# Two of four pairs of memory values made during the norms between layers, and the SSD gate unit moved between the two output halves

## What is computed

```python
for layer in range(DEPTH):
    kind, idx = layer % N_MIXERS, layer // N_MIXERS
    g = P['norm_g'][layer]
    h = rms_norm(x, g[0])
    ...
    x = x + rms_norm(y, g[1])
    h = rms_norm(x, g[2])
    y = memory_cross_attn(h, mem_k[layer], mem_v[layer], P['x_w_q'][layer], P['x_w_o'][layer])
    x = x + rms_norm(y, g[3])

def memory_kv(mem, g, w_k, w_v):
    m = rms_norm(mem, g)
    shp = mem.shape[:2] + (X_HEADS, X_HEAD_DIM)
    return (m @ w_k).reshape(shp), (m @ w_v).reshape(shp)
```

## Time and profile before

| | |
|---|---|
| median of 3 runs | 2404.57 us (2403.11 to 2412.82) |
| the profiled execution, its own time | 2406.28 us |
| its span in the profile | 2404.5 us |
| mean granted TensorE clock | 0.905 of full speed |
| PE, POOL, DVE, ACT busy | 92%, 52%, 53%, 41% of the span |
| DMA | 321.35 MB, 134 GB/s over the span |

### The profile page before, as it was taken

The page is one execution under the profiler, slowest core; times in us unless marked ns, Lnnn a source line. Parts: engine busy times, 40 slices in busy tenths (PEclk is TensorE's granted clock), DMA queues, the critical chain, the costliest instruction groups (busy, mean ns, idle before and its releaser), DMA issues.

```text
span 2404.5 us, 37822 instructions
## 1 busy us (share of the span) xinstructions
PE 2215.2 (92%) x14852; PEld 2014.2 (84%) x14852; DVE 1270.4 (53%) x2173; ACT 980.6 (41%) x1585; POOL 1245.1 (52%) x1565
## 2 busy tenths in 40 slices
PE   6899999789999999899799999999899889989997
PEld 5888997688899997797698889888799679889976
DVE  5798334246666675434245555555233428983342
ACT  3677433423344432333433223332143347774422
POOL 4798881343344452471363334444377039988812
PEclk8999999988899997799898888888799999999998
DMA  3444576143334323376223332333366524435760
GB/s 112 148 123 132 177 242 204 48 118 99 92 113 124 110 92 109 125 245 203 79 88 108 108 107 86 97 98 100 122 205 230 179 76 139 134 118 176 250 202 26
DMA packets 329760, 321.35 MB, mean 134 GB/s; under 512 B 21512, under 2 KB 311216, under 8 KB 329584
## 3 DMA queue, kind: packets, MB, share of 16 engines
q1 hardware_dynamic: 328720, 318.60, 41.7%
q10 hardware_dynamic: 864, 0.34, 0.1%
HBM read 289.27 MB, written 29.61 MB: 133 GB/s over the span
## 4 chain that ended last, share of the span: by engine, by line
PE 65%; DVE 18%; ACT 5%; DMA 5%; issue 3%; POOL 1%; SPq 1%; ACTq 0%; DVEq 0%
PE ps L677 10%; PE ps L678 9%; PE ps L682 9%; PE ps L1208 4%; PE ps L687 3%; PE ps L667 3%; PE ps L668 3%; PE ps L669 3%; PE ps L1084 2%; DVE work L2071 2%; PE ps L1253 2%; PE ps L945 2%; PE ps L954 2%; DVE work L1921 2%; POOL wl L1403 1%
## 5 line engine op out<-in xcount | busy, mean ns | idle before, releaser
L1403 POOL TENSOR_TENSOR wl<-raw,wh 128x256 fp32r<-128x256 f32 x1536 | 1240.6, 843 | 1124.2 <-ACT wh L1426 1123.0
L677 PE MATMUL ps<-Hh,wh 128*128 128x320 f32 (+1 forms) x1536 | 488.0, 334 | 57.5 <-DVE Hl L1967 26.1
L1426 ACT ACTIVATE wh<-raw 128x1024 fp32r<-128x1024 f32 (+1 forms) x400 | 399.7, 1020 | 331.1 <-DMA raw<-hg_w_in 85.1
L678 PE MATMUL ps<-Hl,wh 128*128 128x320 f32 (+1 forms) x1536 | 473.1, 324 | 0.0
L677 PEld LDWEIGHTS ps<-Hh,wh 128*128 128x128 f32 x1536 | 315.4, 205 | 82.0 <-issue 47.9
L678 PEld LDWEIGHTS ps<-Hl,wh 128*128 128x128 f32 x1536 | 317.3, 207 | 1.3
L1921 DVE TENSOR_SCALAR work<-ps 128x512 f32<-128x512 f32 (+9 forms) x248 | 116.1, 486 | 272.2 <-PE ps L1100 56.1
L682 PE MATMUL ps<-Hh,wl 128*128 128x320 f32 (+1 forms) x1536 | 254.7, 309 | 2.8 <-POOL wl L1403 2.8
L682 PEld LDWEIGHTS ps<-Hh,wl 128*128 128x128 f32 x1536 | 233.5, 193 | 4.1 <-POOL wl L1403 4.1
L667 PE MATMUL ps<-Oh,wh 128*128 128x320 f32 x512 | 168.9, 330 | 9.1 <-POOL wl L1403 5.0
L668 PE MATMUL ps<-Ol,wh 128*128 128x320 f32 x512 | 164.8, 322 | 0.0
(11 more groups left out here) (406 smaller groups left out, 4112.4 us busy)
## 6 DMA issues: line engine op xcount, KB each, us to landing
raw<-rg_w_in SPq DMA_DIRECT2D x128, 256.0 KB, 3.7
raw<-hg_w_in SPq DMA_DIRECT2D x128, 256.0 KB, 5.0
raw<-ssd_w_in SPq DMA_DIRECT2D x96, 256.0 KB, 3.8
work<-cache_mem_k SPq DMA_DIRECT2D x40, 512.0 KB, 6.5
raw<-rg_w_out SPq DMA_DIRECT2D x64, 256.0 KB, 3.6
raw<-x_w_k SPq DMA_DIRECT2D x64, 256.0 KB, 3.6
raw<-x_w_v SPq DMA_DIRECT2D x64, 256.0 KB, 5.5
raw<-x_w_q SPq DMA_DIRECT2D x64, 256.0 KB, 3.6
```

Of the source, the lines that this page charges most:

```text
L677: pe.matmul(ps[:, bank, 0:n], high(half, k), mh[:, k, 0:n], start=(k == 0), stop=False)
L678: pe.matmul(ps[:, bank, 0:n], high(half, k), ml[:, k, 0:n], start=False, stop=False)
L1403: ins = pool.tensor_tensor(out, src, wh[:, n % HALVES, r:r + 2].bitcast(F32), ALU.subtract)
L1426: act.activation(wh[:, n % HALVES, 0:rows], raw[:, slot, 0:rows, half * P:(half + 1) * P], ACT.Copy).then_inc(hi_ready, 1)
```

## The change

Layers 1 to 3 get the first two of their four value pairs (`AHEAD = 2`) at the end of the layer before:

- **Units.** Each attention but the last is followed by 4 units (`NEXT_AT`), the two pairs of the next layer; attentions of layers 1 to 3 have 28 of their own. The places move by 4.
- **The early memory norm.** After the attention's last cache block is used, DVE scales the memory rows by the next layer's gains and makes `Hl`; ACT makes `Hh` inside its loop over the output units. The full memory norm stays where it was.
- **The pairs.** PE runs pair 0 (bank 4) behind the sums of the first norm, then four sums of the second, the first half of pair 1 (bank 5), four sums, the second half. ACT copies each to `at_ahead` and the next `high` waits until both are used.
- **DRAM.** SP stores the two pairs to `mv` during the next mixer (`store_ahead`) and loads them back into `at_v` in the next attention. Before it no value weights are put for heads 0 and 1.
- **Attention of layers 1 to 3.** Pairs 2 and 3 alone; the sums of the query norm stand behind pair 2.
- **SSD.** PE: `outputs(j, 0)` ahead of `take_z(i, 1)`. DVE: fading and `outputs(j, 0)` ahead of the gate.
- Waits that keep the shared places apart (`at_ahead_read`, `at_ahead_out`, `at_ahead_back`). Norms are numbered by functions in place of `3 * L + ...`; this alone changes nothing.

The core of the diff:

```diff
+MIX_UNITS = 8 * GROUPS
+MIX_AT = [0, 100, 196, 308]
+OUT_AT = 260
+ATT_AT = [64, 164, 276, 372]
+AHEAD = 2
+QUERY_AT = [80, 176, 288, 384]
+NEXT_AT = [96, 192, 304, 400]
...
+def values_of(L):
+    return range(AHEAD if L else 0, XH)
...
         @block.sync
...
+            def store_ahead(L):
+                sp.wait_ge(*past("at_ahead_read", AHEAD * L))
+                sp.dma_start(RES["mv"][L, 0, :, 0:AHEAD, :].rearrange("(a p) h d -> p a (h d)", p=P), at_ahead).then_inc(S("at_ahead_out"), 16)
...
                 for n in range(EARLY):
                     cache(n)
+                if layer:
+                    sp.wait_ge(*past("at_ahead_out", 16 * layer))
+                    sp.dma_start(at_v[:, :, 0:256 * AHEAD], RES["mv"][layer, 0, :, 0:AHEAD, :].rearrange("(a p) h d -> p a (h d)", p=P)).then_inc(S("at_ahead_back"), 16)
                 for h in range(XH):
-                    put(cols_of(A["x_w_v"][layer], h * 256))
+                    if h in values_of(layer):
+                        put(cols_of(A["x_w_v"][layer], h * 256))
                     sp.wait_ge(*past("at_k_ready", layer * XH + h + 1))
                     sp.dma_start(RES["mk"][layer, 0, :, h, :].rearrange("(a p) d -> p a d", p=P), at_k[:, h % 2]).then_inc(S(f"at_k_out{h % 2}"), 16)
...
+                if layer < DEPTH - 1:
+                    for h in range(AHEAD):
+                        put(cols_of(A["x_w_v"][layer + 1], h * 256))
...
         @block.tensor
...
+                    if j >= 0:
+                        outputs(j, 0)
                     if projects:
                         take_z(i, 1)
                     if j >= 0:
-                        outputs(j, 0)
                         outputs(j, 1)
...
-                for p in range(XH):
-                    values(p)
-                    if p == 0:
+                for p in values_of(L):
+                    pe.wait_ge(*past("at_kvt_ready", KD * L + p + 5))
+                    values(p, p)
+                    if p == values_of(L)[0]:
                         turn_memory(3)
                         sum_squares(3 + 4 * L, 7)
...
                 if L < DEPTH - 1:
-                    sum_squares(5 + 4 * L, 7)
+                    pe.wait_ge(*past("h_ready", KD * (ahead_norm(L + 1) + 1)))
+                    values(0, 4)
+                    for k in range(4):
+                        sum_square(5 + 4 * L, 7, k)
+                    values(1, 5, (0,))
+                    for k in range(4, KD):
+                        sum_square(5 + 4 * L, 7, k)
+                    values(1, 5, (1,))
...
         @block.scalar
...
+                q0 = QUERY_AT[L]
                 ahead(a0 + KD + 2)
                 root(3 + 4 * L, 7)
                 ahead(a0 + KD + 4)
-                high(3 * L + 2)
-                ahead(a0 + KD + 6)
-                ahead(a0 + KD + 8)
+                high(query_norm(L), out=Oh)
+                ahead(q0 - 2)
+                ahead(q0)
...
                 for t in range(KD):
-                    upto(a0 + 24 + t + 2)
-                    act.wait_ge(used, a0 + 24 + t + 1)
+                    upto(q0 + KD + t + 2)
+                    if L < DEPTH - 1:
+                        high_part(ahead_norm(L + 1), t, memh, Hh, NMEM)
+                    act.wait_ge(used, q0 + KD + t + 1)
...
                 root(4 + 4 * L, 6)
                 if L < DEPTH - 1:
+                    def take_ahead(p):
+                        act.wait_ge(used, NEXT_AT[L] + 2 * p + 2)
+                        act.activation(at_ahead[:, :, 256 * p:256 * p + 256], ps[:, 4 + p, :].rearrange("p (a d) -> p a d", a=2), ACT.Copy).then_inc(S("at_ahead_read"), 1)
                     x_squares(2 * L + 1)
+                    take_ahead(0)
+                    ahead(NEXT_AT[L] + 2)
                     root(5 + 4 * L, 7)
-                    high(3 * L + 3)
+                    high(mixer_norm(L + 1), free=NEXT_AT[L] + 4)
+                    take_ahead(1)
+                    ahead(NEXT_AT[L] + 4)
...
         @block.vector
...
                     pack(i)
-                    gate(i)
                     if j >= 0:
                         fade(j)
                         outputs(j, 0)
+                    gate(i)
+                    if j >= 0:
                         outputs(j, 1)
...
+                if L < DEPTH - 1:
+                    wait("at_kb_used", 32 * L + 32)
+                    memory_norm(L + 1, ahead_norm(L + 1), memh)
                 residual(4 + 4 * L, gain(L, 3))
```

More of the change, by code:

```diff
@@ L50, with ahead_norm, mixer_norm, memory_norm_of @@
 EXP_SET = "natural_log_exp_and_others"
[L53 to L56, removed]
+MIX_UNITS = 8 * GROUPS
[5 more added lines that the diff above has]
+NEXT_AT = [96, 192, 304, 400]
+def ahead_norm(L):
+    return 4 * L - 1
+def mixer_norm(L):
+    return 4 * L
+def memory_norm_of(L):
+    return 4 * L + 1
+def query_norm(L):
+    return 4 * L + 2
+def values_of(L):
+    return range(AHEAD if L else 0, XH)
+def values_count(L, p):
+    return L * (XH - AHEAD) + p + 1 if L else p + 1
 N_UNITS = 400
@@ L423, in rg @@
                 u(1)
-                sp.wait_ge(*past("h_ready", KD * (1 if l == 0 else 10)))
+                sp.wait_ge(*past("h_ready", KD * (mixer_norm(3 * l) + 1)))
+                if l:
+                    store_ahead(3)
                 if l == 0:
@@ L746, in take_ri @@
                     pe.wait_ge(*past("rg_u_ready", g0 + i + 1))
+                    if l and i == 0:
+                        pe.wait_ge(*past("at_ahead_read", 3 * AHEAD))
                     if g0 + i:
@@ L771, in take_out @@
                     done(mm)
-                fresh.append(KD * (0 if l == 0 else 9))
+                fresh.append(KD * mixer_norm(3 * l))
                 take_u(0)
@@ L1197, in memory, with values @@
                     project(n % 4, n % 2, n=NMEM)
-                def values(p):
-                    halves(2)
-                    pe.wait_ge(*past("at_kvt_ready", KD * L + p + 5))
+                def values(p, bank, parts=(0, 1)):
+                    if 0 in parts:
+                        halves(2)
                     both, rest_of = pair(), pair_low()
-                    for a in range(2):
+                    for a in parts:
                         at = slice(a * P, (a + 1) * P)
@@ L1456, in root, with high_part, high @@
                 act.activation(rs[:, 0:width], rs[:, 0:width], ACT.Exp, scale=-0.5).then_inc(S("rs_ready"), 1)
-            def high(n, free=None):
+            def high_part(n, k, src, out, width=NT):
+                act.wait_ge(*past("h_full", KD * n + k + 1))
+                act.activation(out[:, k, 0:width], src[:, k, 0:width], ACT.Copy).then_inc(S("h_high"), 1)
+            def high(n, src=Y, out=Hh, width=NT, free=None):
                 if free is not None:
@@ L1463, in high @@
                 for k in range(KD):
-                    act.wait_ge(*past("h_full", KD * n + k + 1))
-                    w = NMEM if n % 3 == 1 else NT
-                    src = (memh if n != 4 else memh_ssd) if n % 3 == 1 else Y
-                    out = Oh if n % 3 == 2 else Hh
-                    act.activation(out[:, k, 0:w], src[:, k, 0:w], ACT.Copy).then_inc(S("h_high"), 1)
+                    high_part(n, k, src, out, width)
             for name, how, tile, r0 in rows:
@@ L1716, in ssd @@
                 ahead(u + 4)
-                high(4, u)
+                high(memory_norm_of(1), memh_ssd, Hh, NMEM, u)
                 squares_of(7)
@@ L1948, in log1p, with normal @@
                 sync()
-            def normal(n, root, src, g, dst=None, width=NT):
-                dst = Y if dst is None else dst
+            def normal(n, root, src, g, dst=Y, width=NT, h=Hh, l=Hl):
                 for k in range(KD):
@@ L2117, in o_low @@
                     wait("rg_o_high", g0 + i + 1)
+                    if l and i == 0:
+                        wait("at_ahead_out", 48)
                     tt(Ol16[:, 2 * i:2 * i + 2, :], rg_o, Oh16[:, 2 * i:2 * i + 2, :].bitcast(F32), SUB).then_inc(S("rg_o_ready"), 1)
-                wait("h_ready", KD * (1 if l == 0 else 10))
+                wait("h_ready", KD * (mixer_norm(3 * l) + 1))
                 for b in range(2):
@@ L2358, in hg @@
                 r16 = restart[:, SEQ:SEQ + 16]
-                wait("h_ready", 7 * KD)
+                wait("h_ready", KD * (mixer_norm(2) + 1))
                 did(dve.memset(hg_A[:, :, 0:1], 0.0))
@@ L2407, in finish @@
                     sync()
+                    if i == 0:
+                        wait("at_ahead_out", 32)
                     did(copy(Oh16[:, 2 * i:2 * i + 2, :], hg_o))
```

80 lines of the change are left out of this document (48 added, 32 removed).

## The result

The changed kernel took **2446.08 us** (median of 4, 2439.66 to 2448.25), the kernel before 2407.78 beside it (4 runs). The ratio is **1.0147**, 95% interval 1.0115 to 1.0179: 38.3 us slower by the medians. The forecast was 2424, 16 to 19 slower; the range ended at 2443, three short of the median. The profiled execution took 2439.66 (span 2437.9), the fastest of the four; the profiled one of before had 2404.5, so 33.4 between the traces.

The account below looks back on a forecast made before the run. PE, busy 92% of the span, bounds the kernel, so time goes where it lacks work or runs at the lower clock. 25 - 1.5 + 14 - 18 = +19.5 gives 2425.8 profiled, 2424 median; range 2392 to 2443.

Parts of the forecast that it names:

- place 2: Attention of layers 1 to 3: a longer chain of weight puts, landings and key copies delays the query units, +14 us.
- Place 1: Norms after layers 0, 1, 2: two pairs moved in start each mixer 8.3 us later, three times, +25 us.
- Normalising takes 4.8: Query norm in layer 2's attention: the step between the root and the first `Ol`, taken as 4.8 us.
- The upper bound of this place, 24: Attention of layers 1 to 3: range 0 to +24 us, by weight landings of 3.7 to 7 us each.
- The wait of 5.1: Norms after layers 0, 1, 2: PE stands 5.1 us in pair 1 until its second unit is split.
- The bound of 9.0: Norms after layers 0, 1, 2: upper bound of each mixer's delay, 9.0 us, with the half pair at half rate.
- Place 3, SSD: SSD groups: reordering shortens PE's stretches at 1.2 GHz, saving 18 us, bounds 0 to -34.
- 3 + 3 + 2 + 4 x 2.7: SSD: savings in us over the seven groups that project and have a group behind them, put at -18.
- the fall behind the small instructions: SSD: clock fall after the 5.8 us stretch of small instructions ahead of the gate unit, charged 1 us.
- The rival in which the chip gives only half of it: SSD: clock falls ahead of the gate unit in every group, SSD gives -9, total +28.5, 2433 us; chance 0.2.
- HGRN: -1.5 forecast: HGRN's first group: four units split at mixer start, not three, so the 1.8 us wait for POOL mostly goes, -1.5.
- The early pairs pay: Attention of layers 1 to 3: value weights arrive in time, first query unit 8.7 us sooner, 2384 us; chance 0.13.

Follow-up runs that it names:

- experiment 3: Changed kernel with SP putting the next weight block ahead of each wait for a key copy in attentions of layers 1 to 3: 2403.62 us, ratio 0.9981.
- experiment 1: Kernel before with only the SSD reordering on PE and DVE, no early pairs: 2392.18 us, ratio 0.9936.
- experiment 9: Changed kernel with ACT's root of the query norm and high-part copies ahead of the splits of the first query units: 2422.97 us, ratio 1.0068.
- experiment 4: Changed kernel with ACT splitting the fourth unit of the early pairs ahead of the squares of the mixer norm: 2436.6 us, ratio 1.0128.
- experiment 2: Changed kernel with the old SSD order, so the early value pairs alone: 2463.15 us, ratio 1.0231.
- one-pair kernel: Changed kernel with one value pair moved ahead in place of two, and SP's weight puts one block earlier: 2369.92 us, ratio 0.9837.

## Why the prediction was right or wrong

- **Direction, and both places of loss: right.** The chain that I had written for place 2 is there link by link, and experiment 3 shows that it is the loss: it is taken away by SP's order alone. The puts came at 1794.1, 1804.4 and 1818.0 in before's time (three links, shifted by the 3.08 that layer 2 starts later), against 1794.2, 1803.6 and 1816.5 forecast.
- **What failed is the sum: +19.5 forecast, +38.3 measured.** The terms of places 1 and 2 were both too small, by 5 and 11 us, for the reasons in the next two points. The holes and the chain were placed right; what follows a hole was priced too low.
- **Place 2 was mis-sized: +14 stood, +25 came.** In layer 2 the first query unit ends 9.6 later against the residual's root, not 3.1. The 6.5 between them: 2.0 until the root (landings of 7.1, 5.9 and 6.5, and the copies behind them); 1.9 until the first `Ol` starts, because the term "Normalising takes 4.8" was the duration of before, when POOL was at the end of its splits, and it took 7.17 beside POOL; 2.6 from there to the end of the unit. Of these 0.7 is a slip of the sum (eight steps that take 7.12 don't fit between 1830.9 and 1836.5; they took 6.28), and 1.9 is the unit behind the last `Ol` at 1.2 GHz (granted clock 0.51), where I had charged 0.5. The upper bound of this place, 24, was passed by 1: I had built it from the landings alone and left the slower norm and the clock out.
- **Place 1 was mis-sized: +25 stood, +30 came** (8.3 forecast a mixer, 9.6 to 10.5 measured). The wait of 5.1 is right to 0.1. The half pair behind it took 4.90, not 3.7, which is 1.2 of the difference each time. In layers 1 and 2 about 1.0 more is the time of before: I had used layer 0's, 10.6 between the two roots, and there it was 9.6. The norm behind it is not a part: it took 3.79 in all three layers, as before. The bound of 9.0, "all of the half pair at half rate", does not come out of its own terms: 7.5 + 2.9 is 10.4, and that would have held all but the last mixer's 10.5.
- **Place 3, SSD, right, and to the tenth by luck:** -18 forecast, -18.0 between the traces, -15.8 by the medians; traces with the old order alone differ by 8 us in this stretch (530.7 to 538.5). The forecast's own terms, 3 + 3 + 2 + 4 x 2.7, make 18.8. The single charges were not right: for the fall behind the small instructions I gave 1 a group, as if it came in some only, and it came in six of the seven gate units, for 3.0 to 3.5 us at half rate, about 1.5 each; behind the second half of the outputs it is 3.5 where I gave 4.5 at most. The rival in which the chip gives only half of it (-9) is out: experiment 1 has -10.6 at the least. The Trainium skill ("TensorE: Matmul & The Clock Gate", section "Part 4: PE-mode transpose") had spoken for that rival, as transposes don't count as work. In this trace the stretch with the four transposes ran at full rate (1.00 over 619.05 to 625.00), and the clock fell behind it, for 3.0 us of the gate unit.
- **HGRN: -1.5 forecast.** The wait for POOL went, but between executions that stretch varies by more than it.
- **"The early pairs pay"** got 0.13 and did not happen, but its mechanism is real: experiment 3 is that rival with its condition as good as met (the second block is split at 1799.18). It gave 2403.6, not 2384. About half of the gap is that a layer's attention gains 7, not 8.7, and the mixers lose 10, not 8.3; the rest lies in the SSD term, HGRN's 1.5 and the median of before, 3 us higher in that group of runs.
- **The range** failed at its upper end by 3 us, and that 3 us is chance. It was built on the median of three runs, 2404.57, so 2443 stood for +38.4; with its fourth run the kernel before has 2407.78, and on that the change is +38.3. But it had left out the worst ends of both places together, and together they came: +30 against 3 x 9.0, +25 against 24. They had a part in common, the low clock behind a hole of PE.

## What to carry to other kernels

Work moved out of a stage moves its loads too, and what stood ahead of a wait in an issuing queue may come to stand behind it. Here that turned a gain of 6 to 8 us a layer into a loss of 7 to 10, and an order of DMA issues put it right. Fill a hole with what fits in it: one pair of matmuls hid behind squares that PE was waiting for anyway, at 0.5 us for 5.8, while the second, at 5.4 for 5.8, went straight onto the path. When several terms of a sum rest on the same assumption, here the clock behind a hole, take their worst ends together.

## What the runs showed of the hardware that I had not expected

- How much DVE's instructions slow down beside POOL's: the same eight normalising instructions took 3.79 us with POOL idle (experiment 9's query norm, and the changed kernel's mixer norms), 4.76 in the query norm of before, where POOL stopped halfway, 5.72 in a mixer norm of experiment 4 and 7.17 in the changed kernel's query norm, with POOL splitting. In experiment 4 single residual steps took 1.02 each while POOL split and 0.54 and 0.48 after it. The Trainium skill ("SBUF — State Buffer", section "SBUF: two separate sides") says that these two share a port pair under an exclusive lock, held for a whole instruction. The rows are in line with it: while DVE's residual steps of experiment 4 followed each other every 0.95, POOL's four instructions beside them took 3.86, 0.97 each. No row shows the lock itself.
- Where the clock falls differs from execution to execution with the same instructions: 140.2 to 145.9 us for one stretch in three kernels that are alike in it. Two profiled executions can differ by 10 us in a stretch that no edit touches, so a part of a few us is read from several kernels, not from one pair of traces.
- The mean granted clock of the whole moved little because two parts of the change pulled it apart: 0.893 with the values alone (experiment 2), 0.910 with the SSD order alone (experiment 1), 0.903 with both and 0.904 in the kernel before, each a mean over its runs. Filling the norm's hole while opening others gave no clock back. The one-pair kernel has 0.914 over its four runs and 0.918 in its trace; the fastest kernel has the highest.
